# The expert stage of a decoder step written out without loops, and one tile's row read from PSUM in the sample's mixer

## What is computed

```python
def peer_ffn(h, wq, subkeys, u_tab, v_tab):        # per block of tokens
    q = (xb @ wq).reshape(PEER_BLOCK, PEER_HEADS, 2, PEER_DKEY // 2)
    s = jnp.einsum('thpd,pkd->thpk', q, subkeys)
    s1, i1 = lax.top_k(s[:, :, 0], PEER_TOPK)
    s2, i2 = lax.top_k(s[:, :, 1], PEER_TOPK)
...
    top_s, sel = lax.top_k(cand, PEER_TOPK)
    idx = jnp.take_along_axis(cidx, sel, axis=-1)
    g = jax.nn.softmax(top_s, axis=-1)
    act = jax.nn.gelu(jnp.einsum('thkd,td->thk', u_tab[idx], xb))
    return jnp.einsum('thk,thkd->td', g * act, v_tab[idx])

def trunk_layer(x, c, ...):
    h = rmsnorm(x, g_mix) * (1 + sc1) + sh1
    mix, new_state = token_mixers(h, w_in, w_out, gate_b, mh_g, sinks, conv_w, state)
    x = x + gt1 * mix
    h = rmsnorm(x, g_ffn) * (1 + sc2) + sh2
    return x + gt2 * peer_ffn(h, wq, subkeys, u_tab, v_tab), new_state
```

## Time and profile before

| | |
|---|---|
| time, median of 3 runs | 2018.54 us (2015.97 to 2029.83) |
| the profiled execution | 2016.57 us, its span 2014.8 us |
| busy: PE, DVE, ACT, POOL | 1579.8, 1208.6, 473.8, 1122.4 us |
| bytes moved | 713.45 MB, 354 GB/s on average |
| gathers of `u` in the mixer | 128 of 512 KB |
| gathers in tiles 1 to 3 of the expert stage | 2 x 384 of 512 KB |
| mean granted TensorE clock | 0.903 of full speed |

### The profile page before, as it was taken

One profiled execution on the slowest core, in us unless ns is written; L12 is line 12 of the kernel. 1 busy time (PEld: TensorE's weight loads), 2 busy tenths in 40 slices (PEclk: granted clock), 3 DMA queues, 4 the chain that ended last, 5 costly groups with the idle time before them and its releaser, 6 DMA issues.

```text
span 2014.8 us, 20816 instructions
## 1 busy us (share of the span) xinstructions
PE 1579.8 (78%) x5461; PEld 746.2 (37%) x5461; DVE 1208.6 (60%) x3129; ACT 473.8 (24%) x1217; POOL 1122.4 (56%) x1168
## 2 busy tenths in 40 slices
PE   6989989987459358768788888698879789799943
PEld 1534546552127013214333344243334334354410
DVE  2223265869767602116667766667776579879973
ACT  1131313121001122212322222223232223332321
POOL 3000020223863545777777667667777767777774
PEclk9989999998775689998999989899999899999966
DMA  9796577798994799999999999999999999999997
GB/s 324 242 362 219 203 257 255 254 376 193 375 382 148 255 412 390 406 413 370 410 420 419 400 368 414 416 342 420 419 402 391 391 378 419 406 419 417 418 367 290
DMA packets 237576, 713.45 MB, mean 354 GB/s; under 512 B 23101, under 2 KB 49055, under 8 KB 237456
## 3 DMA queue, kind: packets, MB, share of 16 engines
q0 software_dynamic: 156672, 570.49, 72.4%
q1 hardware_dynamic: 80488, 140.73, 19.7%
q10 hardware_dynamic: 312, 1.07, 0.2%
HBM read 704.42 MB, written 8.25 MB: 354 GB/s over the span
## 4 chain that ended last, share of the span: by engine, by line
PE 18%; DMA 17%; DVE 10%; POOL 8%; issue 8%; ACT 3%; DVEq 0%; POOLq 0%; ACTq 0%
PE ps_y L2357 12%; DMA v_rows<-in_peer_v_dram,expert_idx_ring 7%; DMA v_rows<-in_peer_v_dram,tile_idx 6%; DVE u_rows L2136 5%; DMA u_rows<-in_peer_u_dram,expert_idx_ring 4%; PE ps_r L2331 4%; POOL u_rows L1916 3%; POOL v_rows L1922 3%; PE ps_y L2385 2%; POOL v_rows L1930 2%; ACT wt_diag L2027 1%; DVE key_scores_w L2147 1%; DVE top_i L2149 0%; DVE top L2148 0%; DVE top_i L2150 0%
## 5 line engine op out<-in xcount | busy, mean ns | idle before, releaser
L2357 PE MATMUL ps_y<-v_rows,wt_diag 128*128 128x512 f32 x1536 | 736.0, 620 | 140.3 <-DMA v_rows<-in_peer_v_dram,expert_idx_ring 75.1
L2357 PEld LDWEIGHTS ps_y<-v_rows,wt_diag 128*128 128x128 f32 x1536 | 285.7, 197 | 529.5 <-issue 515.6
L2136 DVE CUSTOM_DVE_ANT_0 u_rows<-u_rows,ps_y 128x1024 f32<-128x1024 f32 x360 | 420.6, 1217 | 70.5 <-DMA u_rows<-in_peer_u_dram,expert_idx_ring 64.4
L1916 POOL DMA_INDIRECT u_rows<-in_peer_u_dram,expert_idx_ring x384 | 369.6, 963 | 155.3 <-issue 92.3
L1922 POOL DMA_INDIRECT v_rows<-in_peer_v_dram,expert_idx_ring x384 | 365.2, 951 | 123.0 <-issue 99.6
L341 POOL DMA_INDIRECT low_rows<-in_peer_u_dram,tile_idx x128 | 165.6, 1294 | 210.3 <-DVE tile_dots L333 123.2
L608 PE MATMUL ps_z<-w_stream,hT 128*128 128x512 f32 (+5 forms) x560 | 245.9, 596 | 25.9 <-DVE hT L784 15.5
L2385 PE MATMUL ps_y<-v_rows,wt_diag 64*64 64x512 f32 x1024 | 134.7, 643 | 57.9 <-DMA v_rows<-in_peer_v_dram,tile_idx 53.7
L333 DVE CUSTOM_DVE_ANT_0 low_rows<-low_rows,tile_rows 128x1024 f32<-128x1024 f32 x128 | 153.2, 1230 | 40.6 <-DMA low_rows<-in_peer_u_dram,tile_idx 40.0
L1930 POOL DMA_INDIRECT v_rows<-in_peer_v_dram,tile_idx x128 | 121.4, 948 | 72.9 <-PE ps_y L2385 45.6
L608 PEld LDWEIGHTS ps_z<-w_stream,hT 128*128 128x128 f32 (+1 forms) x560 | 99.9, 183 | 150.5 <-issue 119.6
(11 more groups left out here) (442 smaller groups left out, 1691.7 us busy)
## 6 DMA issues: line engine op xcount, KB each, us to landing
w_stream<-in_w_in_dram SPq DMA_DIRECT2D x25, 2048.0 KB, 11.6
w_stream<-in_ada_w_dram SPq DMA_DIRECT2D x12, 2048.0 KB, 12.9
w_stream<-in_peer_wq_dram SPq DMA_DIRECT2D x8, 1024.0 KB, 8.3
wq<-in_peer_wq_dram SPq DMA_DIRECT2D x4, 2048.0 KB, 42.4
w_stream<-in_w_in_dram SPq DMA_DIRECT2D x5, 1568.0 KB, 9.6
w_stream<-in_w_in_dram SPq DMA_DIRECT2D x5, 1536.0 KB, 11.0
u_rows<-in_peer_u_dram,expert_idx_ring POOLq DMA_INDIRECT x384, 8.9
v_rows<-in_peer_v_dram,expert_idx_ring POOLq DMA_INDIRECT x384, 9.0
```

Of the source, the lines that this page charges most:

```text
L1916: g.indirect_dma_start(u_rows[:, j, :], None, U, bass.IndirectOffsetOnAxis(where[:, j:j + 1], 0))\
L2136: v.tensor_tensor_reduce(u_rows[:, j, :], u_rows[:, j, :], row[:, :], 1.0, 0.0, ALU.mult, ALU.add, dots[:, par, j:j + 1]).then_inc(s["u_us ...
L2357: mm = nc.tensor.matmul(ps_y[:, c * 512:(c + 1) * 512], diag[:, par, j, :], v_rows[:, j, c * 512:(c + 1) * 512], start=(first and j == 0), ...
```

## The change

There are two parts. First, the four `Fori` loops of the expert stage (and the two inner ones) become Python loops: the same instructions are written out once per trip, registers and branches go, and every wait has a constant. Second, 95 of the 128 dots of tile 0, namely the last 6 of tile 3 and all 89 of the sample tile, read `h0` from PSUM. `row_to` copies the 128 x 1024 row into two adjoining PSUM banks, three times, each time into a pair that the mixer leaves free: `ps_n` from `behind_rows` to K, `ps_z` for L and N, `ps_n` again for O and Z. To free `ps_z` early, ACT copies the sample's OZ chunk out at once (`act_oz`) and applies the sigmoid later in SBUF; POOL then waits for `oz_ready`. PE gets two waits for `a_used`, ahead of the window scores and of the output product. Two semaphores of the constants are merged.

```diff
+        self.row = X.h0[:, :]
...
-            self.nc.vector.tensor_tensor_reduce(self.rows[:, k % NB, :], self.rows[:, k % NB, :], self.X.h0[:, :], 1.0, 0.0,
+            self.nc.vector.tensor_tensor_reduce(self.rows[:, k % NB, :], self.rows[:, k % NB, :], self.row, 1.0, 0.0,
...
+    def row_to(self, chain, banks):
+
+        self.row = banks[:, :, :].rearrange("p a n -> p (a n)")
+        chain(self.nc.vector.tensor_copy(self.row, self.X.h0[:, :]))
...
-        self.ps_z = [ps("ps_z0", [P, 512]), ps("ps_z1", [P, 512])]
+        self.ps_z01 = ps("ps_z", [P, 2, 512])
+        self.ps_z = [self.ps_z01[:, 0, :], self.ps_z01[:, 1, :]]
...
-        T.pool_og(pool)
+        T.pool_og(pool, oz_copied=True)
...
         T.act_front(act, chain)
+        T.act_oz(act)
...
         def behind_rows(eng):
 
+            eng.wait_ge(before["piece_out"], len(PIECES))
+            X.ahead.row_to(chain, X.ps_n01)
             left(eng)
             T.gap(eng, "A")
...
+        T.z_out(dve, OZ)
+        X.ahead.row_to(chain, X.ps_z01)
         T.gap(dve, "L")
...
+        dve.wait_ge(s["int_ready"], 1)
+        X.ahead.row_to(chain, X.ps_n01)
         T.gap(dve, "O")
...
         T.t_out(pe, S_K1)
+        pe.wait_ge(before["a_used"], DOTS_AT[("sample", "L")])
...
+        pe.wait_ge(before["a_used"], DOTS_AT[("sample", "O")])
         T.out_product(pe, lambda eng: T.on(eng, "oa_ready"), lambda eng: T.t_out(eng, S_HM))
...
-                with pool.Fori(0, LT - 1) as t:
+                for t in range(0, LT - 1):
...
-                with act.Fori(0, LT - 1) as t:
-                    with act.Fori(1, PPT - 3) as p:
+                for t in range(0, LT - 1):
+                    for p in range(1, PPT - 3):
...
-                with dve.Fori(0, LT - 1) as t:
+                for t in range(0, LT - 1):
...
-                with pe.Fori(0, LT - 1) as t:
-                    with pe.Fori(1, PPT - 2) as p:
+                for t in range(0, LT - 1):
+                    for p in range(1, PPT - 2):
```

More of the change, by code:

```diff
@@ L114, in __init__ @@
         self.ident_ready, self.cleared, self.dist_ready = sem("const_ident"), sem("const_cleared"), sem("const_dist")
-        self.sdist_ready, self.s_step = sem("const_sdist"), sem("const_s_step")
+        self.s_step = sem("const_s_step")
         self.pool_ready = sem("const_pool")
@@ L129, in constants_dve @@
         v.memset(C.cols[h * NS:(h + 1) * NS, 1:2], -SLOPES[h])
-    dve.wait_ge(C.sdist_ready, 1)
+    dve.wait_ge(C.dist_ready, 1)
     v.tensor_tensor(C.tpat[:, :], C.tpat[:, :], K["ident"][:, :], ALU.mult).then_inc(C.s_step, 1)
@@ L139, in constants_dve @@
         .then_inc(C.s_step, 1)
-    dve.wait_ge(C.dist_ready, 1)
+    dve.wait_ge(C.dist_ready, 2)
     for h in range(AH):
@@ L192, in constants_pool @@
     g.tensor_copy(C.sdist[:, :], C.sdist_i[:, :])
-    g.tensor_copy(C.tpat[:, :], C.tpat_i[:, :]).then_inc(C.sdist_ready, 1)
+    g.tensor_copy(C.tpat[:, :], C.tpat_i[:, :]).then_inc(C.dist_ready, 1)
     g.tensor_copy(C.dist[:, :], C.dist_i[:, :]).then_inc(C.dist_ready, 1)
-    pool.wait_ge(C.dist_ready, 1)
+    pool.wait_ge(C.dist_ready, 2)
     for h in range(AH):
@@ L526, in __init__ @@
         self.ps_t, self.ps_m = ps("ps_t", [P, 4, P]), ps("ps_m", [P, 512])
-        self.ps_z = [ps("ps_z0", [P, 512]), ps("ps_z1", [P, 512])]
+        self.ps_z01 = ps("ps_z", [P, 2, 512])
+        self.ps_z = [self.ps_z01[:, 0, :], self.ps_z01[:, 1, :]]
         self.ps_s = ps("ps_s", [P, 2, 512])
-        self.ps_n = [ps("ps_n0", [P, 512]), ps("ps_n1", [P, 512])]
+        self.ps_n01 = ps("ps_n", [P, 2, 512])
+        self.ps_n = [self.ps_n01[:, 0, :], self.ps_n01[:, 1, :]]
         self.u = self.g7[:, 0:CW]
@@ L544 @@
            "o_full x1_ready x1_stored state_out pool_done act_step dve_step oz_ready").split()
-PROMPT_ONLY = "w_out_in init upd_full state_ready swa_full x1_stored state_out pool_done oz_ready inter_ready".split()
+PROMPT_ONLY = "w_out_in init upd_full state_ready swa_full x1_stored state_out pool_done inter_ready".split()
 ADA_SIGNALS = ("ada_c_in c_sgm c_silu ct_ps ct_ready picks bias_in gain_in part_full part_out row_full row_ready row_out0 row_out1 "
@@ L1587, in on_scalar @@
         a(intT, X.ps_n[1][:, 0:P], ACT.Copy).then_inc(s["int_ready"], 1)
-        T.act_norm(act, chain, X.ps_t[0:NS, :, :], lambda eng: T.t_landed(eng, S_I), "t_free")
+        T.act_norm(act, chain, X.ps_t[0:NS, :, :], lambda eng: T.t_landed(eng, S_I), "t_free", oz_copied=True)
         T.on(act, "pv_full")
```

## The result

The changed kernel takes 1997.88 us (median of 4 runs, 1996.05 to 1999.42), the kernel before 2019.47 us (4 runs beside them, 2015.97 to 2029.83): a ratio of 0.9884, 95% interval 0.9847 to 0.9921, or 1.2% faster. Its profiled execution took 1997.88 us, with a span of 1996.1 us. 1996 was predicted. Whether the 22 us were saved where the prediction says is another matter, and the page already says that they weren't, in part.

A forecast was written before the change was run, and what follows sets the result against it. It saw memory mostly at 390 to 420 GB/s from slice 14, with holes in the mixer and at DVE's loop jump, and POOL's gathers costliest. Terms -9.4 - 3 - 3.5 - 2.2 - 4.3 = -22.4 us gave 1996; 8-in-10 range 1984 to 2009.

The forecast's parts named there:

- one of its own signs: Sample tile: the prediction is wrong if PE's C comes at 605 us in spite of shorter gathers.
- The jump: Expert stage, end of the loop's first trip: DVE's 9.43 us wait goes; -9.4 us, bounds 7 to 12.4.
- Register arithmetic: Expert stage's loop tiles: waits on computed values become waits on constants; -3 us for both tiles, bounds 0 and -10.
- Start of the sample tile: Mixer, 490 to 603 us: shorter gathers fill two holes, less one copy, reaching the end through C's load; -3.5 us.
- The middle: Mixer, 603 to 656 us: a chain of PE and DVE, second copy covered by a wait for rows; nothing gained.
- O: Mixer from 656.93 us: the first gather's delay goes, dots end at 672.4 instead of 674.63 us; -2.2 us.
- Z: Mixer's last eleven dots: gathers at 0.94 us land just in time, end 689.8 instead of 694.1 us; -4.3 us.
- New waits: Sample tile: PE's waits for K's and N's dots and DVE's for ACT's OZ copy cost nothing, 0.5 us at worst.
- transfers set the mixer: Rival, chance 0.17: faster gathers only take memory time from weights and caches, C lands as before; -14.4 us, 2004.
- more than that: Rival, chance 0.12: DVE keeps POOL waiting in both loop tiles, mixer's start and jump give more; -36 us, 1982.5.
- The rule that speaks against the change: Mixer's gathers: the skill's port table infers dots with two SBUF inputs and descriptor generation use different interfaces and wouldn't meet.

## Why the prediction was right, and where it wasn't

The sum was right (-22.4; -21.6 by medians). Its parts were not all right, and by one of its own signs it was wrong: it called itself wrong if PE's C came at 605 us in spite of short gathers, and PE got it at 614.88, or at 608.5 if the 6.4 us of the later start are taken off. From the mixer's last dot to the end the two traces differ by 21 us and not by some 12. Of its terms:

- **The jump**, -9.4: 9.8 to 11.5 at the edge (52.9 us less the 43.1 of the two kernels in which only DVE's loop is gone or doesn't jump, or less the 41.4 of all nine), inside its bounds of 7 to 12.4. The reason held: one backward jump, DVE's, behind which it waits for code.
- **Register arithmetic**, -3: 7.6 + 0.4. Mis-sized. I took DVE's slack as covering most of it; where DVE is late, its 1.8 us for each pair of groups show. Its name was at best half right too, since on DVE's program the no-operations behind the waits are nearly all of it, and only DVE's count.
- **Start of the sample tile**, -3.5: 0. This step failed. I let faster gathers bring C forward "through the load of the state C", with memory as what sets it. They bring C's issue forward, by 4.3 us, but C then waits in its queue's order, behind small packets that advance one for one with the gathers' packets, and takes 5.3 us longer. C in takes 130.1, 130.8 and 129.9 us with the row in PSUM, 125.4 to 133.4 without.
- **The middle**, put at nothing: 47.6 us from C in to O's start in the three kernels with all rows in PSUM and the old queues (46.8 to 48.1), 49.9 in the five without (48.6 to 51.6): -2.3. One way in which it can come is the wait for `z_o` behind N's long gathers, which one of the five has, with 3.7 us; what it is in the other four is open.
- **O**, -2.2: 17.35 us from O's start to the residual (mean of eight, the copy included) against 17.82 (mean of six): -0.5. The 3.4 us from the first dot to the first gather I took for the same blocking. From the reading of the dot's sum they are 3.44 or 3.45 us in all fourteen executions, whatever the row's place: not blocking by dots. In the traces of the kernel before and of the changed one POOL's other gathers behind idle stretches of 8 to 35 us start 0.8 to 1.0 us after the event that releases them. What the 3.4 are is open.
- **Z**, -4.3: its dots take 12.6 us in all eight executions with the row in PSUM, and 12.96 to 18.45, mean 16.0, in the six without: -3.4; against the five of these with the old queues (mean 16.6) -4.0. The mechanism held, and what the row in PSUM takes away is above all the chance of a gather of 4 to 6.5 us.
- **New waits**, 0: none shows.

With the old queues the mixer's parts, 0, -2.3, -0.5 and -4.0, make up its 6.6 us. The loops gave 19.5 where 12.4 were forecast, the row 6.6 where 10 were. Of the rivals, "transfers set the mixer" had the right observation, that C lands as before, and "more than that" was right on DVE in the loop; the errors of the two parts cancelled in good part. So that the time was met so closely was luck: two terms were wrong in opposite directions, one was overlooked, and 6 us of scatter with the clock hid part of it in the one pair of traces. The rule that speaks against the change (gather and dot wouldn't meet) doesn't hold here: with both inputs in SBUF 33 to 41 of the mixer's 87 gathers behind 480 us take over 1.3 us, up to 6.55; with the row in PSUM none or one, up to 1.45.

## What to carry to other kernels

Ask of a wait for a transfer what stands ahead of it in its own queue, in packets and not in bytes: a load behind 2048 small packets moves at the pace of the other queues' packets, and a queue of its own costs two lines. When a loop's engine is the late one, look at its jump back and at what each wait on a register adds; write out that engine's loop first, and see whether the others are worth it. And part a change in experiments even when the forecast time is met.

## What the runs showed of the hardware

- Two full DMA queues advanced packet for packet: 1138 of 3.7 KB to 1144 of 1.6 KB on average in 15 us.
- DVE's jump back left it idle for 4.5 to 9.4 us and cost 9.8 to 11.5 at the edge; a branch that wasn't taken cost nothing. Each of the seven halts behind the jump, of 4.8 to 5.4 us, ended 1.82 to 1.85 us after the start of an 8 KB packet of the instruction queue.
- A no-operation behind a wait cost DVE 0.05 us; over a block of keys and one of pairs, 1.6 us.
- The first gather after POOL's idle stretch ahead of O started 3.44 us after the reading of the dot that freed its buffer, in every kernel; the gathers behind it follow at 0.30.
- The granted clock of one untouched stretch of PE was 0.98 in one execution and 0.93 in another, and the next stage began 6 us later in the second.
